# Odd mixer entry: expert rows combined on TensorE with diagonal matrices, per-tile square sums, five gather buffers

## The reference, cut to what matters

```python
# end of layer 0: each token takes its two experts' rows, weighed, and adds them gated
y = einsum("tkd,tk->td", ys[dest].reshape(T, TOP_K, D), w)   # T = 1280, TOP_K = 2, D = 1024
x = x + gate * y
# start of layer 1
h = rmsnorm(x, g) * (1 + scale) + shift
z = h @ w_in_cd                   # 1024 -> 1536 columns: ux, ug, up, 512 each
ux, ug, up = split(z)             # ux also for the 256 context tokens
lat = [multiscale_pool(up), rglru(conv(ux)) * gelu(ug)]
# merge: rmsnorm of both branches, then @ w_out
```

## Time and profile before

| | |
|---|---|
| median of 3 runs | 2456.19 us (2454.78 to 2459.57) |
| the profiled execution, its own time | 2464.21 us |
| span of the profile | 2462.4 us |
| mean granted TensorE clock | 0.935 of 2.4 GHz |
| TensorE busy | 2186.4 us (89%) |
| VectorE, ScalarE, GpSimd busy | 778.8, 648.7, 180.6 us |
| odd mixer's block | from about 1403 to 1707 us of the span |

### The profile page before, as it was taken

How to read it: one execution, slowest core, us unless ns; L and a number is a source line. 1 busy time by engine, 2 the same in 40 slices (tenths; PEclk the granted TensorE clock), 3 DMA queues, 4 the chain that set the end, 5 groups by cost and what they waited for, 6 DMA issues and landing times. The chain is left out here.

```text
span 2462.4 us, 36052 instructions
## 1 busy us (share of the span) xinstructions
PE 2186.4 (89%) x15594; PEld 1111.6 (45%) x15594; DVE 778.8 (32%) x1292; ACT 648.7 (26%) x1049; POOL 180.6 (7%) x126
## 2 busy tenths in 40 slices
PE   6999989968985999999999679996986999988884
PEld 5788875545663333333333234443762333322222
DVE  6333336654225111111111162665642111111004
ACT  5311025552214111111111153664331111111111
POOL 0010000000000000000000121352000000000003
PEclk8999999989997999999999889998997999999986
DMA  9101025038924989889999450001108999999995
GB/s 365 28 26 43 26 112 238 1 103 286 292 75 183 424 357 399 357 351 408 418 414 420 130 176 26 21 22 43 35 31 348 411 413 421 409 416 416 428 408 214
DMA packets 147922, 596.97 MB, mean 242 GB/s; under 512 B 25556, under 2 KB 63152, under 8 KB 123056
## 3 DMA queue, kind: packets, MB, share of 16 engines
q1 hardware_dynamic: 117648, 516.47, 52.9%
q0 software_dynamic: 11952, 43.52, 4.7%
q10 hardware_dynamic: 18160, 34.61, 3.8%
HBM read 535.84 MB, written 58.72 MB: 241 GB/s over the span
## 5 line engine op out<-in xcount | busy, mean ns | idle before, releaser
L1869 PE MATMUL ph<-w,x_t 128*32 128x512 f32 x6016 | 684.5, 608 | 39.9 <-DMA w<-in_exp_w 37.7
L1869 PEld LDWEIGHTS ph<-w,x_t 128*32 128x32 f32 x6016 | 191.7, 112 | 455.3 <-issue 426.7
L1982 DVE TENSOR_TENSOR hidden<-hidden,ph 64x512 f32<-64x512 f32 x94 | 102.3, 1088 | 759.8 <-ACT hidden L1940 759.8
L1882 PE MATMUL py<-w,g_t 128*32 128x512 f32 x3008 | 341.2, 594 | 1.0 <-DVE g_t L1988 1.0
L1940 ACT ACTIVATE hidden<-ph 64x512 f32<-64x512 f32 x94 | 55.6, 591 | 699.0 <-PE ph L1869 699.0
L2205 PE MATMUL z<-hT,w_cd 128*128 128x512 f32 (+1 forms) x448 | 186.4, 574 | 5.2 <-ACT hT L2242 5.2
L1882 PEld LDWEIGHTS py<-w,g_t 128*32 128x32 f32 x3008 | 94.0, 110 | 204.6 <-issue 203.3
L747 PE MATMUL z<-h_high,w_hi 128*128 128x512 f32 (+1 forms) x432 | 161.7, 374 | 14.6 <-DVE h_low L832 10.8
L1847 POOL DMA_INDIRECT x_rows<-h_tokens,index x47 | 44.4, 945 | 1766.6 <-PE px L1854 985.0
L748 PE MATMUL z<-h_low,w_hi 128*128 128x512 f32 (+1 forms) x432 | 158.1, 366 | 0.0
L749 PE MATMUL z<-h_high,w_lo 128*128 128x512 f32 (+1 forms) x432 | 157.4, 364 | 0.0
(11 more groups left out here) (330 smaller groups left out, 2379.2 us busy)
## 6 DMA issues: line engine op xcount, KB each, us to landing
w<-in_exp_w SPq DMA_DIRECT2D x192, 2048.0 KB, 16.4
ada_raw<-in_ada_w SPq DMA_DIRECT2D x21, 2048.0 KB, 8.2
y_slots<-y_rows ACTq DMA_DIRECT2D x188, 128.0 KB, 9.0
y_slots<-zero SPq DMA_DIRECT2D x29, 512.0 KB, 15.4
h_tokens<-h_rows ACTq DMA_DIRECT2D x18, 512.0 KB, 2.8
w_ab<-in_w_in_ab SPq DMA_DIRECT2D x14, 512.0 KB, 3.8
w_cd<-in_w_in_cd SPq DMA_DIRECT2D x14, 512.0 KB, 3.7
ada_first<-in_ada_w SPq DMA_DIRECT2D x3, 2048.0 KB, 17.6
```

The lines of the kernel that those rows point to most:

```text
L1869: ins = pe.matmul(ph[row:row + UNIT, :], xt[:, k, at:at + UNIT], w13[place[2 * b + n] % RING][:, half, k, :], start=(k == 0), stop=(k == K ...
L1882: ins = pe.matmul(py[b % 2][row:row + UNIT, :], gt[:, k, n * UNIT:(n + 1) * UNIT], w2[place[2 * b + n] % RING][:, k, half * 512:(half + 1) ...
L1982: dve.tensor_tensor(hid[PAIR:P, :].rearrange("s (k q) -> s q k", k=FT), hid[0:PAIR, :].rearrange("s (q k) -> s q k", k=FT), ph[PAIR:P, :]. ...
```

## The change

1. `scale` and `added` are gone. VectorE builds per tile two diagonal 128 x 128 matrices, the identity times the token's weights (`diagonals`, one instruction). TensorE's `turn` multiplies, for each of 8 blocks, the stationary block of `y_a` with the first diagonal and that of `y_b` with the second, and adds both in PSUM: 16 products in place of 8 transposes.
2. There are five gather buffers in place of three. They lie with the diagonals over the recurrence's buffers.
3. The sums of squares are made per tile: the squared block is stationary, a column of ones moves (8 products per tile). `copy_rows` and `fold` are gone.
4. The orders of TensorE, ScalarE and VectorE are written anew; `between` as well. ScalarE executes a Sqrt on one column first.
5. The first units are ux0, up0 and ug0 of chunk 0, then ux0 of chunks 1 and 2, up0 and ug0 of chunk 1. Unit count and sizes are the same. SyncE loads the first three `w_cd` blocks before the small gate and pool weights.
6. The multiplies with the gelu are done in halves of 512 tokens, those of branches 0 to 2 before the last scans.

The diff, cut to its core:

```diff
-        EARLY = 2
-        tiles = [("ug", i, (0,)) for i in range(EARLY)]
+        tiles = []
         for i in range(BR):
-            tiles += [("ux", i, (0, 1, 2)), ("up", i, (0, 1))]
-        tiles += [("ug", i, (0, 1)) for i in range(EARLY, BR)] + [("ug", i, (1,)) for i in range(EARLY)]
-        unit = [(m, i, kind, c) for m, (kind, i, parts) in enumerate(tiles) for c in parts]
+            tiles += [("ux", i, (0, 1, 2)), ("up", i, (0, 1))] + [("ug", i, (0, 1))] * (i == 0)
+        tiles += [("ug", i, (0, 1)) for i in range(1, BR)]
+        early = [(m, i, kind, 0) for m, (kind, i, parts) in enumerate(tiles[:3])]
+        unit = early + [(m, i, kind, c) for m, (kind, i, parts) in enumerate(tiles) for c in parts if c or m >= len(early)]
...
-        NB = 3
+        NB = 5
...
                 def turn(t):
-                    pe.wait_ge(c_wb, t + 1)
+                    pe.wait_ge(c_dg, t + 1)
+                    pe.wait_ge(s_ya[t % NB], 16 * (t // NB + 1))
+                    pe.wait_ge(s_yb[t % NB], 16 * (t // NB + 1))
                     if t >= 2:
                         pe.wait_ge(c_x, t - 1)
                     for k in range(KT):
-                        ins = pe.transpose(turned[t % 2][:, k * P:(k + 1) * P], yb[:, t % NB, k * P:(k + 1) * P], self.c("ident"))
+                        for c, y in enumerate((ya, yb)):
+                            ins = pe.matmul(turned[t % 2][:, k * P:(k + 1) * P], y[:, t % NB, k * P:(k + 1) * P], dg[:, t % NB, c, :],
+                                            start=(c == 0), stop=(c == 1))
                     ins.then_inc(c_t, 1)
...
+                def row_sums(t):
+                    pe.wait_ge(c_sq, t + 1)
                     for k in range(KT):
+                        ins = pe.matmul(row_ps[:, t:t + 1], hT[:, k, t * P:(t + 1) * P], self.c("ones", 1),
+                                        start=(k == 0), stop=(k == KT - 1))
                     ins.then_inc(c_sum, 1)
...
+                between = {(0, 3): ((row_sums, 5), (turn, 7)), (0, 7): ((row_sums, 6), (turn, 8)),
+                           (1, 3): ((row_sums, 7), (turn, 9)), (1, 7): ((spread, 1),), (2, 3): ((row_sums, 8),),
+                           (2, 7): ((row_sums, 9),), (3, 3): ((spread, 2),)}
+                turn(0)
+                turn(1)
+                for t in range(2, 5):
                     turn(t)
+                    row_sums(t - 2)
+                row_sums(3)
                 turn(5)
+                spread(0)
+                row_sums(4)
                 turn(6)
...
             @block.scalar
+                act.activation(stat[:, 3, 0:1], self.c("ones", 1), ACT.Sqrt)
                 for t in range(4):
                     square(t)
+                root_of_mean(0)
+                modulated(0, range(KT // 4))
                 square(4)
+                modulated(0, range(KT // 4, KT // 2))
                 square(5)
+                modulated(0, range(KT // 2, KT))
                 square(6)
                 square(7)
                 evict(0)
+                root_of_mean(1)
+                modulated(1, range(KT // 2))
                 square(8)
+                modulated(1, range(KT // 2, KT))
                 evict(1)
                 square(9)
+                root_of_mean(2)
                 evict(2)
                 modulated(2, range(KT))
...
             @block.vector
+                def diagonals(t):
+                    if t >= NB:
+                        dve.wait_ge(c_t, t - NB + 1)
+                    dve.tensor_tensor(dg[:, t % NB, :, :], self.c("ident").unsqueeze(1).to_broadcast([P, 2, P]),
+                                      self.wgt[:, :, t:t + 1].to_broadcast([P, 2, P]), ALU.mult).then_inc(c_dg, 1)
...
+                for t in range(NB):
+                    diagonals(t)
                 for t in range(5):
                     new_x(t)
+                    diagonals(t + NB)
                 mean(0)
                 inverse(0)
                 scaled(0, range(KT // 2))
+                new_x(5)
+                scaled(0, range(KT // 2, KT))
                 new_x(6)
                 new_x(7)
                 new_x(8)
                 mean(1)
+                inverse(1)
+                scaled(1, range(KT // 2))
                 new_x(9)
+                scaled(1, range(KT // 2, KT))
...
+                gated(0)
                 under_root(BR - 1, 1)
+                for i in range(1, BR - 1):
+                    gated(i)
                 scans(BR - 1, 1)
                 both_ways(BR - 1)
-                for i in range(BR):
-                    dve.tensor_tensor(self.Y[:, BR + i, :], self.Y[:, BR + i, :], total[i], ALU.mult).then_inc(s_y, 1)
+                gated(BR - 1)
```

More of the change, by code:

```diff
@@ L2043, in odd_mixer @@
         ug_order = [(i, c) for m, i, kind, c in unit if kind == "ug"]
-        tail = [n for n, (m, i, kind, c) in enumerate(unit) if kind == "ug" and n >= EARLY]
+        tail = [n for n, (m, i, kind, c) in enumerate(unit) if kind == "ug" and i]
         gates_at, roots_at, pool_at, pool_in = {}, {}, {}, {}
@@ L2065, in odd_mixer @@
             xl = self.sb(ctx, "x_conv", [P, L])
[L2066 to L2073, removed]
+            stat = self.sb(ctx, "x_stats", [P, 4, NT])
             with ExitStack() as same_place:
                 ya = self.sb(same_place, "y_a", [P, NB, D])
+                yb = self.sb(same_place, "y_b", [P, NB, D])
+                dg = self.sb(same_place, "weight_diagonals", [P, NB, 2, P])
+            lanes = [[self.sb(ctx, f"lru{d}{n}", [P, L]) for n in range(3)] for d in range(2)]
+            sqr = self.sb(ctx, "a_squared", [P, L])
             kept = self.sb(ctx, "lru_total", [P, BR - 1, SEQ])
@@ L2124, in _ @@
                     sp.dma_start(w[:, m % NW, :, :], W[:, :, at:at + P]).then_inc(s_w[m % NW], 16)
+                    if m == len(early) - 1:
+                        sp.wait_ge(s_zero, 1)
+                        for d in range(2):
+                            for gate, name in enumerate(("lru_wa", "lru_wx")):
+                                for par in range(2):
+                                    sp.dma_start(gw[par * HD:(par + 1) * HD, d, gate, :, par * HD:(par + 1) * HD],
+                                                 self.i[name][0, d, par::2, :, :].rearrange("i h j -> h i j")).then_inc(s_gw, 16)
+                        sp.dma_start(pw[:], self.i["pool_w"][0].rearrange("g i j -> i g j")).then_inc(s_pw, 16)
             @block.tensor
@@ L2193, in _ @@
                 for n, (m, i, kind, c) in enumerate(unit):
-                    if n == EARLY:
+                    if n == len(early) + 1:
                         pe.wait_ge(s_gw, 16 * 8)
                         pe.wait_ge(s_pw, 16)
-                    if c == tiles[m][2][0]:
+                    if c == 0:
                         pe.wait_ge(s_w[m % NW], 16 * (m // NW + 1))
@@ L2202, in _ @@
                     for k in range(KT):
-                        if n == 0 or kind == "ux" and i == 0 and c:
+                        if kind == "ux" and i == 0:
                             pe.wait_ge(c_h, KT * c + k + 1)
@@ L2363, in mean @@
                 def mean(c):
-                    dve.wait_ge(c_sum, c + 1)
-                    dve.tensor_scalar(stat[:, 0, part[c][0]:part[c][-1] + 1], row_ps[:, 0:len(part[c])], 1.0 / D, EPS,
-                                      ALU.mult, ALU.add).then_inc(c_var, 1)
+                    dve.wait_ge(c_sum, part[c][-1] + 1)
+                    here = slice(part[c][0], part[c][-1] + 1)
+                    dve.tensor_scalar(stat[:, 0, here], row_ps[:, here], 1.0 / D, EPS, ALU.mult, ALU.add).then_inc(c_var, 1)
                 def inverse(c):
@@ L2449, in both_ways, with gated @@
                     dve.tensor_tensor(total[i], total[i], lanes[1][1][:, 0:SEQ], ALU.add).then_inc(s_sum, 1)
+                def gated(i):
+                    dve.wait_ge(s_sum, i + 1)
+                    for c in range(2):
+                        here = slice(c * 512, (c + 1) * 512)
+                        dve.wait_ge(s_ug, ug_order.index((i, c)) + 1)
+                        dve.tensor_tensor(self.Y[:, BR + i, here], self.Y[:, BR + i, here], total[i][:, here], ALU.mult).then_inc(s_y, 1)
                 for i in range(BR):
```

80 lines of the change are left out of this document (6 added, 74 removed).

## The result

The changed kernel takes **2465.86 us** (median of 8 runs, 2462.23 to 2470.97) against 2455.49 us for the kernel before (8 runs, 2451.61 to 2459.57): ratio 1.0037, with a 95% interval of 1.0024 to 1.005. It is 10.4 us slower. The sign of the forecast and its range hold, and 2463.1 us is 2.8 us off. The rise itself was forecast at 6.9 us, 3.5 less than it is.

What follows compares the result with a forecast made beforehand. It took TensorE's work up to the fifth unit to bound the kernel: +11.4 to the first unit, -1.1 to the fifth, -3.4 at the end, so 2456.2 + 6.9 = 2463.1 us, range 2453 to 2471.

Steps and rivals of the forecast that it cites:

- Start: TensorE's first turn: waits for the gather, not an add, but three loads go ahead; taken at 1413.0, as before.
- Rival A: Entry: gather at 1411.7, full clock 2 us sooner, no cold stretch after square(4); sum +2.8, 2459 us; chance 0.26.
- First turn: TensorE's first turn runs at clock 0.50, full clock once it is done; cost 3.4 us.
- Price of a turn and of a sum: TensorE: a diagonal turn takes 32 x 0.11 = 3.5 us at full clock, a tile's sum 1.8 us.
- rival B: Turns: a diagonal product costs a transpose, turn 1.8 us, TensorE no longer the bound; sum -15, 2441 us; chance 0.10.
- Rival C: Turns: second record's weight load shows, or columns move at a quarter of transpose rate; +26 to +35 us; chance 0.06.
- The new wait: TensorE idles 3.4 us between spread(0) and row_sums(4), as square(4) stands behind two modulations on ScalarE.
- The clock behind it: One stretch at 0.50 follows the wait before row_sums(4); 1.7 us, bounds 0 and 3.4.
- Second part: First unit to the fifth unit's end: 52.5 us at full clock, 1.3 idle at row_sums(8), against 53.6; -1.1 us.
- After the fifth unit: The same units, gates and pool products follow; no change put, 1 us if the convolution's cover is gone.
- The end: After VectorE's last sum only the last branch's multiply (1.3 us) remains of 4.7; merge's first square earlier, -3.4 us.
- GpSimd: Gathers in the entry: with five buffers no request waits, the 3.85 us wait for a buffer goes.

Runs made afterwards that it cites:

- e3: The kernel before with only the new end (gelu multiplies in halves, most ahead of the last scans); 2450.35 us, one run, against 2457.18.
- e5: The kernel before with five gather buffers in place of three; 2455.04 us, one run, against 2459.48.
- e4: The changed kernel with the old weighing (scale, add, eight transposes) and square(4) and square(8) ahead of the modulations; 2446.17 us, ratio 0.9959.
- e6: e4 with the sums of squares per chunk, copies and folds as in the kernel before; 2434.14 us, ratio 0.9905.
- e8: e4 with 13 unused 512-column products added on TensorE around the first turns and sums; 2433.81 us, one run, against 2459.48.
- e9: e6 with unused products, eight before the first turn and one after each of turns 0 to 4; 2430.97 us, ratio 0.99.
- e7: The changed kernel with four unused 512-column products between spread(0) and row_sums(4); 2459.98 us, one run.
- e1: The changed kernel with square(4) and square(8) moved ahead of the modulations of chunks 0 and 1; 2456.45 us, ratio 1.0001 to the kernel before.
- e2: The changed kernel with one product per block, the second expert's row left out of the sum; 2529.5 us, one run, block 20.6 us shorter.

## Why the prediction came out as it did

**Start.** Right, as the sum of two terms that cancelled. The first turn came 9.96 us after the block's start, before 10.05. The wait for the gather itself won its 1.28 us, but the first gather landed 1.3 us later: 9.97 us after the start, before 8.71. The experiments bear this out: with the old order of SyncE's loads it landed at 8.1 and 8.2 us (e3, e5), with the new one at 10.0 to 10.3 (e4, e6, e8, e9). So the new order of loads cost 1.3 to 2 us, and no run varies it alone. Rival A, with the gather at its earliest and no stretch at half clock behind the wait, is out.

**First turn.** Right in kind. The lower clock lasted 5.2 us of it, a loss of 2.6; 3.4 was put.

**Price of a turn and of a sum.** Right. A turn took 3.57 us (forecast 3.5), a tile's sum 1.79 to 1.84 (1.8). Two records per product it is (x2 on each line), each at 0.112 us, so rival B is out. Rival C's first form is out too: the second record's weight load doesn't show beyond that. (C's extra cost for the turns, 26 to 35 us, would have come on top of the 6.9, which its total leaves out.) Eight transposes take 0.91 us from their start to that of the next work (e6, 1430.67 to 1431.58), 0.114 each; a float32 product of the same shape takes 3.57/16 = 0.223. By the rows a product costs twice a transpose. The Trainium skill, "TensorE: Matmul & The Clock Gate", section "Terms", names a factor of 4 for FP32; the measurement differs, and decides.

**The new wait.** Right: 3.4 forecast, 3.28 on the row. e7, which fills it, and e1, which removes it, both show it where the prediction put it. (The terms given there, 0.7 + 2 x 0.73 + 1.06, add up to 3.2 and not 3.4.)

**The clock behind it.** The mechanism was right, the size was the upper bound: 6.8 us at 0.50, a loss of 3.4 where 1.7 was put. e7 measured it alone: 3.42 us.

With these the first part closes: 2.6 + 7 x 3.57 + 5 x 1.79 + 0.5 + 3.3 + 3.4 = 43.8 us from the first turn to the first unit, measured 43.7.

**Second part.** Here a step failed. Forecast -1.1 us, measured +2.5 (53.9 to 56.3). The wait at `row_sums(8)` was there as worked out (1.3 forecast, 1.25 measured), but the sum took everything after the first unit "at full clock", while 6.8 us at 0.50 followed that wait, a loss of 3.4 us. The prediction gave this shorter wait no clock of its own. Why the clock fell there is not settled. In the windows above TensorE is busy 2.15 of the 3.40 us ahead of the drop, 1.4 of them with one-column records. The same happened in e7 (wait 1.25). But in e2 the same wait of 1.26 us, with the same half unit ahead and the same 16 records behind it, was followed by none. A wait of 0.97 us there was followed by none in e1 and e4 and by 3.4 us at half clock in e8. So neither the wait nor the work beside it decides it, and no run filled this wait by itself. That the half clock is what this part lost is shown, by the rows; what brought it is open.

**After the fifth unit.** Right: no change. It took 202.07 us against 202.06. The window behind the fifth unit, for comparison with the last of the earlier trace rows:

```profile
1508.00:1710.00 202.00, 192.95 (x479) 91.32 (x478) 115.22 (x65) 112.18 (x139) 84.73 (x34) 0.98 0.08 24
```

**The end.** Right: -3.4 forecast, -3.2 measured. That e3 gives 2.7 by the same edit is explained by the half of branch 1 that it must keep.

**The merge.** Not in the prediction: from the merge's first square to its first product 15.5 us against 17.0. ScalarE waits there for a load of the merge's weights, 3.48 us in the changed kernel and 4.92 before (`w_o`, L1261 of its timeline), and the distance was 15.4 to 17.0 us in the kernels of this study, none of which touches the merge. I don't put it down to the change.

**GpSimd.** Wrong, off the path. It was forecast without a wait for a buffer, and still waits in the changed kernel, on its timeline:

```profile
1414.09 0.94 POOL L2464 DMA_INDIRECT y_a<-y_slots,slot  x1 [3.25 <-PE pa L2134]
```

A turn that takes 3.6 us (the first, with its cold part, 6.1) frees buffers more slowly than gathers are issued, so five buffers fill too. With TensorE as the bound this costs nothing; in e5, where it isn't, the first unit came 2.9 us earlier with the two more buffers.

**The sum.** Forecast 11.4 - 1.1 - 3.4 = +6.9; measured 12.6 + 2.5 - 3.2 - 1.4 = +10.4 (the unrounded terms, 12.58, 2.46, -3.22 and -1.43, give 10.39). The two terms that were missed are both the clock: 1.7 us in the first part, 3.4 in the second. Against them stood 0.8 us less of it in the first turn, and the merge's 1.4, which the prediction did not have; that the time came within 2.8 us of the forecast is in part luck.

## What to carry to other kernels

Moving elementwise work to TensorE did not pay here, since the added products outlasted the waits they filled and TensorE became what the entry waits for. Price the products in records, and set them against the idle time they are to fill, before choosing. Where an engine's list puts work that waits for TensorE ahead of work TensorE waits for, look at that one place first: here two squares, one line each, cost about as much as the whole loss. And a record with one moving column took as long as one with 128 (0.112 us at full clock), so the sums over many tokens were cheaper with the data as the moving operand (e6).

## What the runs showed of the hardware that was not expected

- TensorE stayed at 0.50 while it was busy 21.51 of 21.80 us with transposes and one-column products (e4), and for 6.7 us of that its work was one-column products alone. In e1 it fell to 0.50 without an idle moment behind 3.6 us of one-column products, but behind the same products in the changed kernel it did not. Products of 512 columns that compute nothing useful brought the turns to 0.94 and took 7.7 us off the block (e8). The Trainium skill, "TensorE: Matmul & The Clock Gate", section "Part 4: PE-mode transpose", says that a transpose doesn't count as a busy TensorE in the same way; e4, at 0.50, fits that. What share the transposes have in e4's low clock was not told apart from the one-column products'.
- Two waits of 3.28 and 1.25 us were each followed by 6.8 us at half clock. The lost 3.4 us is as much as the longer wait itself, and filling it gave them back (e7). Behind the shorter it came in two kernels (after, e7) and stayed away in a third (e2), and behind one of 0.97 us it came in e8, for 3.4 us, and stayed away in e1 and e4.
- A kernel that beats both came out of the parts: five buffers, the new order of units and of the end, the old weighing and the sums per chunk (e6, ratio 0.9905). Filler adds nothing measurable to it (e9, 0.99).
- The DMA engines moved 359 GB/s at a busy share of 1.07 with three gather buffers and 380 at 1.05 with five, over 17 us of the entry (before, e5): a full busy share did not mean the highest rate.
